# The second norm's vector: from the normed rows to each expert's turned rows

## The reference

```python
def rms_norm(x, g):
    y = xf * lax.rsqrt(jnp.mean(xf * xf, axis=-1, keepdims=True) + EPS)
    return y * g

xp = xp + moe_ffn(rms_norm(xp, ffn_norm_g[l]), *moe_w)

# in moe_ffn: coarse top-1 of 4 groups, top-2 of 8 experts in that group
grp_logits = xt @ w_group + b_group
exp_logits = xt @ w_router + b_router
...
xb = x_pad[tok_b]                                      # rows of one expert
hb = jax.nn.silu(xb @ w_gate_e[e]) * (xb @ w_up_e[e])
out = (hb @ w_down_e[e]) * gate_b[:, None]
```

## Time and profile before

| | us |
|---|---|
| median of three runs | 1095.88 |
| span of the profiled execution (no other time of it is given) | 1089.4 |
| TensorE matmul busy | 859.8 |
| VectorE busy | 388.8 |
| ScalarE busy | 201.3 |
| GpSimd busy | 325.3 |

### The profile page before, as it was taken

How to read it: one execution, slowest core, us unless ns; L and a number is a source line. 1 busy time by engine, 2 the same in 40 slices (tenths; PEclk the granted TensorE clock), 3 DMA queues, 4 the chain that set the end, 5 groups by cost and what they waited for, 6 DMA issues and landing times.

```text
span 1089.4 us, 13673 instructions
## 1 busy us (share of the span) xinstructions
PE 859.8 (79%) x5197; PEld 586.5 (54%) x5197; DVE 388.8 (36%) x571; ACT 201.3 (18%) x304; POOL 325.3 (30%) x239
## 2 busy tenths in 40 slices
PE   1999988449999999799429888888788778778860
PEld 1999888449999999799113333222222223223220
DVE  4206999986458454511750000000000000000008
ACT  4323212032212432212400100000000000000003
POOL 2234999025424414411410111111011101111104
PEclk9999989769999999899759999999999999999985
DMA  7423121012223222351939999999999999999935
GB/s 217 143 79 107 47 78 39 1 60 68 97 66 103 63 78 96 102 193 77 387 105 403 372 408 420 420 419 421 420 420 419 421 420 421 420 421 418 421 147 214
DMA packets 73515, 262.26 MB, mean 241 GB/s; under 512 B 8743, under 2 KB 42691, under 8 KB 48352
## 3 DMA queue, kind: packets, MB, share of 16 engines
q1 hardware_dynamic: 68368, 252.96, 59.2%
q0 software_dynamic: 5120, 8.93, 2.2%
HBM read 256.60 MB, written 13.74 MB: 248 GB/s over the span
## 4 chain that ended last, share of the span: by engine, by line
PE 37%; DMA 25%; DVE 19%; issue 11%; POOL 4%; ACT 3%; SPq 1%; DVEq 0%; POOLq 0%; ACTq 0%
DMA gu<-in_w_up_e 24%; PE ps L814 14%; DVE work L1143 11%; PE ps L587 10%; PE ps L628 5%; POOL w_low L1445 4%; PE ps L835 4%; DVE xh L1103 1%; PE ps L561 1%; DVE xh L1414 1%; DMA xh<-in_x_prompt 1%; PE ps L803 1%; DVE xh L1406 1%; PE ps L672 1%; ACT w_high L885 1%
## 5 line engine op out<-in xcount | busy, mean ns | idle before, releaser
L1445 POOL TENSOR_TENSOR w_low<-ring,w_high 128x2048 fp32r<-128x2048 f32 (+1 forms) x38 | 155.5, 4092 | 236.6 <-ACT w_high L885 236.4
L587 PE MATMUL ps<-x_high,w_high 128*128 128x272 f32 x640 | 175.6, 292 | 7.3 <-POOL w_low L1445 7.3
L1372 DVE COPY work<-ps 128x512 f32<-128x512 f32 x32 | 22.1, 692 | 440.8 <-PE ps L803 440.8
L587 PE MATMUL ps<-x_low,w_high 128*128 128x272 f32 x640 | 174.2, 290 | 0.0
L1143 DVE SCALAR_TENSOR_TENSOR work<-slot,param,work 128x512 f32<-128x512 f32 x240 | 162.6, 752 | 1.2 <-DVE work L1200 1.2
L1532 POOL DMA_INDIRECT expert_rows<-xx,idx_now x32 | 32.8, 1025 | 387.0 <-ACT xx L1058 355.4
L587 PE MATMUL ps<-x_high,w_low 128*128 128x272 f32 x640 | 133.8, 291 | 0.0
L814 PE MATMUL ps<-gu,work 128*64 128x512 f32 x512 | 118.4, 617 | 19.4 <-DMA gu<-in_w_up_e 18.5
L814 PE MATMUL ps<-slot,work 128*64 128x512 f32 x480 | 112.9, 625 | 18.7 <-issue 18.0
L587 PEld LDWEIGHTS ps<-x_high,w_high 128*128 128x128 f32 x640 | 121.9, 191 | 8.6 <-issue 4.6
L587 PEld LDWEIGHTS ps<-x_low,w_high 128*128 128x128 f32 x640 | 121.7, 190 | 0.0
(11 more groups left out here) (240 smaller groups left out, 1080.0 us busy)
## 6 DMA issues: line engine op xcount, KB each, us to landing
ring<-in_w_down_e SPq DMA_DIRECT2D x16, 2048.0 KB, 22.1
gu<-in_w_gate_e SPq DMA_DIRECT2D x16, 2048.0 KB, 18.0
gu<-in_w_up_e SPq DMA_DIRECT2D x16, 2048.0 KB, 23.3
slot<-in_w_gate_e SPq DMA_DIRECT2D x15, 2048.0 KB, 17.5
slot<-in_w_up_e SPq DMA_DIRECT2D x15, 2048.0 KB, 22.8
slot<-in_w_down_e SPq DMA_DIRECT2D x15, 2048.0 KB, 22.4
ring<-in_w_in SPq DMA_DIRECT2D x22, 1024.0 KB, 5.1
ring<-in_w_out SPq DMA_DIRECT2D x4, 1024.0 KB, 8.2
```

The lines of the kernel that those rows point to most:

```text
L587: last = pe.matmul(ps[:, 2 * r + half, 0:HT], w[:, k, c * P:(c + 1) * P], part[:, k, half * HT:(half + 1) * HT], start=(k == 0 and len(par ...
L1372: v.tensor_copy(xgT[s].rearrange("p c m -> p (c m)"), ps[:, s]).then_inc(xgT_ready, 1)
L1445: g.tensor_tensor(w_low[s][:, 0:kt], wring[s][:, 0:kt], w_high[s][:, 0:kt].bitcast(F32), ALU.subtract).then_inc(low_ready, 1)
```

## The change

`g` is no longer multiplied into the normed rows. GpSimd's loop L1509 goes; the normed rows are stored as ScalarE leaves them, and SP's stores wait for ScalarE directly. VectorE's copy of the turned rows becomes a multiplication with `gain`, a new tile of eight numbers per partition, of which each serves 64 columns. `gain` is loaded once near the start; the broadcast load of `ffn_row` goes.

```diff
+    gain = sb("gain", [P, 2, 4])
...
-    ffn_row = final_row = late_rows[:, 0:D]
+    final_row = late_rows[:, 0:D]
...
         for dst, src in late:
             sp.dma_start(dst, src).then_inc(late_loaded, 16)
+        sp.dma_start(gain[:], d["ffn_norm_g"][0].rearrange("(h p c) -> p h c", h=2, c=4)).then_inc(gain_loaded, 16)
...
                 sp.dma_start(x[0:NS, 4], d["x_sample"].rearrange("b i n -> (b i) n")).then_inc(x_again, 16)
-                sp.dma_start(ffn_row, d["ffn_norm_g"][0].partition_broadcast(P)).then_inc(norm_rows_loaded, 16)
...
-            nc.scalar.activation(xn2[0:n, c], x[0:n, c], ACT.Identity, scale=stat[0:n, 60 + c:61 + c]).then_inc(h_scaled, 1)
+            nc.scalar.activation(xn2[0:n, c], x[0:n, c], ACT.Identity, scale=stat[0:n, 60 + c:61 + c]).then_inc(xn2_done, 1)
...
-            v.tensor_copy(xgT[s].rearrange("p c m -> p (c m)"), ps[:, s]).then_inc(xgT_ready, 1)
+            v.tensor_tensor(xgT[s].rearrange("p c (h m) -> p c h m", h=2), ps[:, s].rearrange("p (c h m) -> p c h m", c=4, h=2),
+                            wide(gain[:].rearrange("p h c -> p c h").unsqueeze(3), [P, 4, 2, CAP]), ALU.mult).then_inc(xgT_ready, 1)
...
+        dve.wait_ge(gain_loaded, 16)
         dve.wait_ge(xn2_stored, 16 * NCH)
...
-        dve.wait_ge(norm_rows_loaded, 32)
+        dve.wait_ge(norm_rows_loaded, 16)
...
-        pool.wait_ge(norm_rows_loaded, 16)
-        for c in range(NCH):
-            n = chunk_rows(c)
-            pool.wait_ge(h_scaled, c + 1)
-            g.tensor_tensor(xn2[0:n, c], xn2[0:n, c], ffn_row[0:n], ALU.mult).then_inc(xn2_done, 1)
```

More of the change, by code:

```diff
@@ L324, in program @@
     rstd_in = sem("rstd_in")
-    h_scaled = sem("h_scaled")
+    gain_loaded = sem("gain_loaded")
     xn2_stored = sem("xn2_stored")
```

## The result

The kernel after ran four times: 1081.43, 1081.64, 1082.83 and 1082.93 us, median 1082.24. Before, with one more run beside these, has a median of 1095.75 us. The ratio is 0.9884, with a 95% interval of 0.987 to 0.9898: 1.2% faster, by 13.5 us in these runs. The forecast was 1086.2 us, 9.65 us less, with a range from 1083.8. The profiled span went from 1089.4 to 1079.4 us, where the prediction had 1079.7.

The account below looks back on a forecast made before the run. The prediction took a serial routing chain along VectorE, slowed by GpSimd's multiplications, to delay the whole expert stage. It subtracted 9.65 us from the median 1095.88 to get 1086.2 us, range 1083.8 to 1089.0.

Parts of the forecast that it names:

- What the change removes: Routing: without GpSimd's five multiplications, seven VectorE steps shrink from 11.53 to 1.88 us, so the chain is 9.65 us shorter.
- What is late next: Routing: ScalarE's exponential, stores and loads ahead of the gather, or TensorE's clock might end last instead; none expected to.
- three covers: Routing: ScalarE has 1 us left, DMA work lands 3 us before the gather, TensorE's clock falls before its next product.
- Rival 1: Expert stage start: first gather runs into loads and takes 6.8 us, eating 3.8 us; 1090.0 us, chance 0.12.
- The multiplication and the moved load: Expert stage and start: multiplication replacing the copy costs up to 0.1 us each, 0.8 for eight; moved load costs 0.
- Rival 3: Expert stage: the new multiplication waits for GpSimd, 1.7 us more each; 1119 us, chance 0.03.
- The sum: Whole kernel: 9.65 us off the 1089.4 span gives 1079.7; off the 1095.88 median, 6.5 above the span, 1086.2 us.
- The range: Whole kernel: 1083.8 to 1089.0 us, a dip and a little more downward, up to the middle of Rival 1.
- one clock dip: TensorE's part of the chain: a down product takes 5.35 instead of 3.65 us; likeliest error, 1084.5 to 1087.9.

Follow-up runs that it names:

- e2: Kernel before with only GpSimd's five multiplications L1509 left out, both loads of the vector kept; 1083.6 us, ratio 0.9902.
- e3: Kernel after with five GpSimd multiplications put back that read the normed rows and write to an unread place; 1091.12 us, ratio 0.9962.
- e9: Kernel after with ten GpSimd memsets beside the routing, which write SBUF but read nothing; median 1084.27 us, ratio 0.9882.
- e4: Kernel after with the plain copy from PSUM in place of the multiplication with gain; 1083.33 us over four runs.
- e5: Kernel after, unchanged, run beside eleven runs of before; median 1083.06 us over six runs, ratio 0.9899.
- e1: Kernel before, unchanged, run again for scatter and trace; median 1094.1 us over thirteen runs, the profiled one 1089.38 us.
- e10_before_b: Kernel before, unchanged, for one more trace; one of two such traces, at 1094.34 and 1094.54 us.

## Why the prediction was wrong

- **What the change removes: right.** 9.65 us forecast, 9.80 measured in the routing. The same shapes at two speeds in one trace were enough to find the neighbour and to price its leaving. e2, e3 and e9 show that the neighbour was the cause.
- **What is late next: right.** Each of the three covers came out: 1.02 us of spare time on ScalarE, 3.4 us of idle DMA ahead of the gather, TensorE at the lower clock level (0.50) well before its next product. Rival 1, a gather among loads, did not come.
- **The multiplication and the moved load: right, at 0.** e4 and e2 show no difference beyond the scatter. Rival 3, a multiplication that waits for GpSimd, did not come once: 690 to 692 ns in 32 of 32.
- **The sum: the step that failed.** "I carry the difference over: 1095.88 - 9.65." The term that was mis-sized is the 1095.88. All sixty runs of before have a median of 1094.6 us and lie between 1089.4 and 1096.9. Two of the three that were shown are, at 1095.88, among the six longest of the sixty, and the profiled execution, 1091.3 us by its span, would be the sixth shortest. That the span stood 6.5 us under the median should have been read as a sign of this. I took it for a constant instead; the constant is 1.9 us. From a typical execution, 1092.5 us of span and 1.9 us around it, less 9.80, the forecast would have been 1084.6 us. So the base explains 1.5 us of the miss of 4.0, and the 0.15 of the saving comes on top. Of the 2.4 us that are left, 0.6 is that the four runs after were faster than the ten (1082.24 against 1082.8); for the rest see the last point. That the spans came out at 1079.7 and 1079.4 is in part luck: the trace after is a short one too, at 36.50 us to the first product and 480.35 in the mixer.
- **The range: too narrow for the same reason.** It had one clock dip, 1.7 us, as its error. The runs of before alone spread over 7.6 us. A part of that is L1103, which has two lengths, 4.2 us apart, by whether GpSimd's first cast starts before or behind its fourth step. The long one (9.27 us for five instructions) stood in the trace, and it was the same lock that I had just explained. It widens the range, but it is not what moved the result: the first trace of before and both traces after have the long form.
- **What stays open.** The runs come in sets, and the mean of before differs from set to set, from 1093.8 to 1095.4 us; so before and after are best compared within one. The means are 13.2 us apart in the set of the result (4 runs and 4; standard error 1.1, if a run scatters as in the larger sets), 10.9 in that of e5 (11 and 6, 0.8), and 10.3 between before and e2 with e4, whose traces differ from after in nothing that shows (35 and 10, 0.5). The routing gives 9.8 us. The two larger sets lie 1.1 and 0.5 us above it, which their errors nearly cover. The first lies 3.4 us above it, three of its errors. No stretch of the four traces of before holds more than the 9.8 beyond its scatter, so I don't know where that set's 3.4 us come from, or whether they would come again.

## What to carry to other kernels

Look in a trace for instructions of one shape at two durations; what ran beside the slow ones is the cost, and a GpSimd instruction that reads SBUF, beside short VectorE steps with two SBUF inputs on the chain, is priced at about its own length for each step that it meets (1.5 to 1.9 us beside 1.89, 2.0 to 2.35 beside 2.38). Before a time is forecast from a span, put the span against the runs: where they do not stand at the usual distance, the profiled execution is not a typical one, and the range has to take in the runs' own spread. Price a late tile by the wait of the engine that needs it, not by how long the tile's own instruction was held up.

## What was not expected of the hardware

- Two executions of one program differ by over 4 us through this lock. What decides is not the cast's own time but which step it meets. Counted from the start of the norming, the cast came at 2.14 us in e1, behind the start of the fourth step, and the five took 5.03 us. It came at 1.75 us in e10_before_b (at 16.26, later on the clock of the trace than e1's 16.16) and at 1.89 in e9, ahead of the fourth step, and the five took 9.27 us.
- A GpSimd multiplication of 128x1024 took 1.89 us with one tile as both inputs and 2.38 with two tiles, and VectorE's steps beside it stood as much shorter. The first also wrote to another tile and the second to one of its inputs; no run tells the two apart.
